# Forms of w_up's result split into high and low parts where they are made, and loaded back as both parts into the tiles that w_down's matmuls read

## What is computed

```python
h2 = rmsnorm(x, norm_mlp_g)
f = relu(einsum('btd,df->btf', h2, w_up))          # 2048 -> 8192
x = x + einsum('btf,fd->btd', f * f, w_down)       # 8192 -> 2048
y = rmsnorm(x, norm_final_g)
```

## Time and profile before

| | before |
|---|---|
| median of three runs | 1854.97 us |
| profiled execution, its own time | 1855.15 us |
| its span | 1853.1 us |
| TensorE busy | 1814.2 us (98%) |
| VectorE busy | 1477.5 us (80%) |
| ScalarE busy | 923.8 us (50%) |
| q1 (weights) | 186.86 MB, 32.6% of 16 engines |
| q0 (POOL's) | 99.18 MB, 18.7% of 16 engines |

### The profile page before, as it was taken

How to read it: one execution, slowest core, us unless ns; L and a number is a source line. 1 busy time by engine, 2 the same in 40 slices (tenths; PEclk the granted TensorE clock), 3 DMA queues, 4 the chain that set the end, 5 groups by cost and what they waited for, 6 DMA issues and landing times. The chain is left out here.

```text
span 1853.1 us, 38289 instructions
## 1 busy us (share of the span) xinstructions
PE 1814.2 (98%) x15016; PEld 1805.6 (97%) x15016; DVE 1477.5 (80%) x2028; ACT 923.8 (50%) x1316; POOL 131.8 (7%) x222
## 2 busy tenths in 40 slices
PE   7999999999999999999999999999999999999997
PEld 6999999999999999999999999899999999999997
DVE  7777785445488888888888888888888888889886
ACT  6545533333344544454454455555555555555554
POOL 2000000200000001000000000110000000000100
PEclk9999999999999999999999999999999999999999
DMA  8333233444345345444444542887666766767632
GB/s 278 97 96 92 91 97 92 127 142 139 113 149 174 133 154 177 151 155 141 166 142 145 174 133 90 246 241 203 182 185 186 199 179 182 198 161 208 206 103 93
DMA packets 209420, 288.21 MB, mean 156 GB/s; under 512 B 9389, under 2 KB 185017, under 8 KB 209248
## 3 DMA queue, kind: packets, MB, share of 16 engines
q1 hardware_dynamic: 185344, 186.86, 32.6%
q0 software_dynamic: 23920, 99.18, 18.7%
HBM read 222.00 MB, written 64.53 MB: 155 GB/s over the span
## 5 line engine op out<-in xcount | busy, mean ns | idle before, releaser
L863 PE MATMUL ps<-forms,u_high 128*128 128x260 f32 x1344 | 379.9, 283 | 2.2 <-ACT u_high L1128 1.2
L865 PE MATMUL ps<-forms,u_low 128*128 128x260 f32 x1344 | 379.5, 282 | 0.0
L864 PE MATMUL ps<-forms,u_high 128*128 128x260 f32 x1344 | 379.2, 282 | 0.0
L863 PE MATMUL ps<-forms,d_high 128*128 128x260 f32 x1120 | 317.1, 283 | 3.1 <-DVE d_low L1737 1.4
L865 PE MATMUL ps<-forms,d_low 128*128 128x260 f32 x1120 | 316.1, 282 | 0.0
L864 PE MATMUL ps<-forms,d_high 128*128 128x260 f32 x1120 | 316.1, 282 | 0.0
L863 PEld LDWEIGHTS ps<-forms,u_high 128*128 128x128 f32 x1344 | 253.0, 188 | 2.5 <-ACT u_high L1128 1.4
L864 PEld LDWEIGHTS ps<-forms,u_high 128*128 128x128 f32 x1344 | 253.4, 189 | 0.0
L865 PEld LDWEIGHTS ps<-forms,u_low 128*128 128x128 f32 x1344 | 252.8, 188 | 0.0
L1277 DVE TENSOR_TENSOR w_low<-raw,w_high 128x512 fp32r<-128x512 f32 x160 | 109.0, 689 | 136.9 <-ACT w_high L941 135.7
L863 PEld LDWEIGHTS ps<-forms,d_high 128*128 128x128 f32 x1120 | 210.7, 188 | 5.1 <-issue 4.3
(11 more groups left out here) (305 smaller groups left out, 4380.3 us busy)
## 6 DMA issues: line engine op xcount, KB each, us to landing
even_rows<-in_w_up_dram SPq DMA_DIRECT2D x32, 1024.0 KB, 5.4
odd_rows<-in_w_up_dram SPq DMA_DIRECT2D x32, 1024.0 KB, 5.7
d_even<-in_w_down_dram SPq DMA_DIRECT2D x33, 768.0 KB, 6.7
d_odd<-in_w_down_dram SPq DMA_DIRECT2D x33, 768.0 KB, 5.2
raw<-in_w_in_dram SPq DMA_DIRECT2D x96, 256.0 KB, 2.7
sums_spill<-part_out POOLq DMA_DIRECT2D x40, 520.0 KB, 5.4
scratch<-f_spill POOLq DMA_DIRECT2D x20, 910.0 KB, 7.1
f_spill<-f_out POOLq DMA_DIRECT2D x32, 520.0 KB, 4.6
```

The lines of the kernel that those rows point to most:

```text
L863: pe.matmul(out, wh[:, k, :], xh, start=(PRODUCT_OPENS[r] and k == 0), stop=False, skip_group_check=True)
L864: pe.matmul(out, wh[:, k, :], xl, start=False, stop=False, skip_group_check=True)
L865: mm = pe.matmul(out, wl[:, k, :], xh, start=False, stop=last, skip_group_check=True)
```

## The change

The forms of a pair are split as soon as they are made. In w_up, split_high (ScalarE, at r = 6) writes the high parts of all seven forms into f_high, a view of scratch; split_low (VectorE, at r = 0 two pairs on) subtracts them in place, so that f_out and the sums tiles hold the low parts. For that f_scale and f_sums stand one turn earlier (r = 4 and 5). POOL stores both parts in f_parts_spill, and loads both straight into f_forms[kp % 8], in two pieces (three and four forms). window_high, window_low, their landing tiles and the lists BUILD and FORMS_AT go. The last pair's forms are made in segments 1 to 3 in place of 3 to 6 (SUMS_SEG = 3). What ScalarE's window_high waited for, POOL's load_forms waits for now. Loads of tiles 0 and 1 stand ahead of send_f(30), those of tiles 2 to 7 directly behind it and ahead of the first send_sums, later ones ahead of the sums of the segment that frees their set.

```diff
+PIECES = ((0, 3), (3, FORMS))
...
-SQUARES_AT, SCALE_AT, SUMS_SEG = first_q(3) + 3, first_q(3) + 6, 6
+SQUARES_AT, SCALE_AT, SUMS_SEG = first_q(1) + 3, first_q(1) + 6, 3
...
-        f_dram = nc.dram_tensor("f_spill", (DOWN_KP, P, FORMS, HALF), F32).ap()
+        parts_dram = nc.dram_tensor("f_parts_spill", (DOWN_KP, P, 2, FORMS, HALF), F32).ap()
+        f_high = scratch[:].rearrange("p k (a t) -> p (k a) t", a=2)[:, 0:FORMS, :]
...
+            def load_forms(kp):
                 if kp == 0:
+                    pool.wait_ge(u_lo, UP_Q - PRODUCTS)
+                elif kp == 1:
+                    pool.wait_ge(u_lo, UP_Q)
+                elif kp < D_SETS:
+                    pool.wait_ge(u_used, UP_Q)
                 else:
+                    pool.wait_ge(u_used, first_q(LAST_USE[kp - D_SETS] + 1))
+                pool.wait_ge(split_sent, 16 * (kp + 1))
                 pool.wait_ge(f_out_sent[kp % 2], SENT[kp])
+                for piece, (first, end) in enumerate(PIECES):
+                    pool.dma_start(f_forms[kp % D_SETS][:, :, first:end, :].bitcast(F32),
+                                   parts_dram[kp, :, :, first:end, :]).then_inc(forms_in[kp % D_SETS][piece], 16)
...
             def send_f(m):
                 pool.wait_ge(f_ready, m + 1)
+                to = parts_dram[m, :, 1]
+                pool.dma_start(parts_dram[m, :, 0], f_high).then_inc(split_sent, 16)
+                pool.dma_start(to[:, 0:4, :], f_out[m % 2][:]).then_inc(f_out_sent[m % 2], 16)
...
             for m in range(UP_PAIRS - 1):
                 if m == UP_PAIRS - 2:
-                    load_f(1)
+                    load_forms(0)
+                    load_forms(1)
                 send_f(m)
-                if m == 8:
-                    load_f(0)
+            for kp in range(2, D_SETS):
+                load_forms(kp)
...
+            for seg in range(FIRST_FINAL):
                 if seg == SUMS_SEG:
                     send_f(UP_PAIRS - 1)
+                for kp in range(D_SETS, DOWN_KP):
+                    if LAST_USE[kp - D_SETS] == seg:
+                        load_forms(kp)
+                send_sums(seg)
...
+                        if FIRST_USE[kp] == m - UP_PAIRS and r < 2:
+                            pe.wait_ge(forms_in[kp % D_SETS][r], 16 * (kp // D_SETS + 1))
...
+            def split_high(m):
+
+                act.wait_ge(f_summed, m + 1)
+                act.wait_ge(split_sent, 16 * m)
+                for part, first, end in split_parts(m):
+                    act.activation(f_high[:, first:end, :].bitcast(F32R), part, ACT.Copy).then_inc(split_hi, 1)
...
+                if r == 6 and 1 <= m < UP_PAIRS:
+                    split_high(m - 1)
+                if turn == first_q(SUMS_SEG) + 1:
+                    split_high(UP_PAIRS - 1)
...
+                if r == 0 and 2 <= m <= UP_PAIRS:
+                    split_low(m - 2)
+                if turn == first_q(SUMS_SEG) + 2:
+                    split_low(UP_PAIRS - 1)
...
+                if 1 <= m < UP_PAIRS and r == 4:
+                    f_scale(m - 1)
                 if 1 <= m < UP_PAIRS and r == 5:
-                    f_scale(m - 1)
-                if 1 <= m < UP_PAIRS and r == 6:
                     f_sums(m - 1)
```

More of the change, by code:

```diff
@@ L96, in first_q @@
     return UP_Q + PRODUCTS * seg
[L100 to L116, removed]
-SQUARES_AT, SCALE_AT, SUMS_SEG = first_q(3) + 3, first_q(3) + 6, 6
+for _kp in range(D_SETS, DOWN_KP):
+    assert LAST_USE[_kp - D_SETS] + 1 < FIRST_USE[_kp]
+SQUARES_AT, SCALE_AT, SUMS_SEG = first_q(1) + 3, first_q(1) + 6, 3
 SENT = {}
@@ L361, in build @@
         d_rows_in = [[sem(f"d_{which}_in{b}") for b in range(4)] for which in ("even", "odd")]
-        f_landed = [sem(f"f_landed{b}") for b in range(2)]
-        f_hi, f_lo = sem("f_hi"), sem("f_lo")
+        f_summed, split_hi, split_sent = sem("f_summed"), sem("split_hi"), sem("split_sent")
+        forms_in = [[sem(f"forms_in{kp}_{piece}") for piece in range(len(PIECES))] for kp in range(D_SETS)]
         sums_sent = [sem(f"sums_sent{b}") for b in range(2)]
@@ L386, in form_rows, with split_parts, split_count @@
             return odd_sums[:, 0, :], odd_sums[:, 1, :], odd_sum[:]
+        def split_parts(m):
+            if m == UP_PAIRS - 1:
+                return (f_out[1][:], 0, 4), (end_sums[:], 4, 7)
+            if m % 2 == 0:
+                return (f_out[0][:], 0, 4), (even_sums[:], 4, 7)
+            return (f_out[1][:], 0, 4), (odd_sums[:], 4, 6), (odd_sum[:].unsqueeze(1), 6, 7)
+        def split_count(m):
+            return 2 * m + m // 2
         def blocks_at(q):
@@ L635, in send_sums @@
                                accum_op=ALU.add).then_inc(sums_sent[seg % 2], 16)
-            loaded = 2
-            for seg in range(-1, FIRST_FINAL):
+            for seg in range(FIRST_FINAL):
                 if seg == SUMS_SEG:
                     send_f(UP_PAIRS - 1)
[L641 to L646, removed]
+                for kp in range(D_SETS, DOWN_KP):
+                    if LAST_USE[kp - D_SETS] == seg:
+                        load_forms(kp)
+                send_sums(seg)
             for i, n in enumerate(FINALS):
@@ L654, in _ @@
                 else:
-                    pool.wait_ge(f_hi, 2 * DOWN_KP)
-                    pool.wait_ge(f_lo, 2 * DOWN_KP)
+                    pool.wait_ge(f_out_sent[0], SENT[UP_PAIRS - 2])
+                    pool.wait_ge(f_out_sent[1], SENT[UP_PAIRS - 1])
                 pool.dma_start(x3[n][:].rearrange("p k (a t) -> p (k a) t", a=2), sums_dram[n]).then_inc(x3_in[i], 16)
@@ L1185, in _ @@
             x2_squares(OUT_PAIRS - 1)
[L1186 to L1199, removed]
             def final_steps(i):
@@ L1817, in f_sums, with split_low @@
                 settle()
[L1818 to L1826, removed]
+                dve.tensor_tensor(s4, a12, s2, ALU.subtract).then_inc(f_summed, 1)
+            def split_low(m):
+                dve.wait_ge(f_summed, m + 1)
+                for n, (part, first, end) in enumerate(split_parts(m)):
+                    dve.wait_ge(split_hi, split_count(m) + n + 1)
+                    if end == FORMS:
+                        settle()
+                    ins = dve.tensor_tensor(part.bitcast(F32R), part, f_high[:, first:end, :], ALU.subtract)
+                    if end < FORMS:
+                        step(ins)
+                ins.then_inc(f_ready, 1)
             def pair_final(i):
@@ L1872, in _ @@
                     f_sums(UP_PAIRS - 1)
-                for part in range(2):
-                    if turn - 2 - part in FORMS_AT:
-                        window_low(FORMS_AT[turn - 2 - part], part)
                 if seg > FIRST_FINAL and r == 3:
```

33 lines of the change are left out of this document (4 added, 29 removed).

## The result

| | before | after |
|---|---|---|
| median of four runs each | 1855.41 us | 1872.44 us |
| lowest to highest | 1853.54 to 1857.82 | 1871.62 to 1873.49 |
| profiled execution (span) | 1855.15 (1853.1) | 1872.58 (1870.8) |

The change makes the kernel slower: ratio 1.0094 (95% interval 1.0081 to 1.0107), some 17 us. The forecast was 1876 in 1863 to 1890.

What follows compares the result with a forecast made beforehand. The prediction took TensorE, busy 1814.2 of 1853.1 us, as the bound, with VectorE limiting for a while early in w_down. Its terms: 1855.15 + 25 - 4 + 0 = 1876 us, range 1863 to 1890.

Steps and rivals of the forecast that it cites:

- w_up: 0: In w_up, the added splits fit VectorE's free 2.8 us a pair, 2.2 wanted, so TensorE loses 0 us.
- The queue: +25: At the seam, 14.9 MB in POOL's queue ahead of segment 0's sums delay the copy waiting for them: +25 us.
- the copy that was named: ScalarE's copy of C11 at r = 5 of segment 2, forecast at 1211.5 against 1186.35 before.
- Given back: -4: Between segments 2 and 7, TensorE catches up 6.2 us less a 2 us stall in segment 3: 4 us returned.
- The stop in segment 3: In w_down, pair 31's f_sums and split now stand in segment 3 on VectorE: 2 us of stall.
- Near the end: 0: Near the end of w_down, 3.6 us of idle may shrink by 1, collisions may take 1: 0.
- possible collisions of double loads: In w_down, two tiles free at once put 3.7 MB in q0; collisions may take 1 us in the forecast.
- rival 1: Later collisions after segments 7, 15, 23 and 31, 3 to 4 us each: 1890 us; chance 0.12.
- Rival 2: At the seam, the sums overtake the loads in q0, and segment 3 waits for rows: 1863 us; chance 0.08.
- rival 3: w_up doesn't hold the splits; 0.5 us a pair lost, 16 us on top: 1891 us; chance 0.06.
- rival 4: Segment 0's sums land before 1186.35 and only VectorE's relief is left, faster: 1849 us; chance 0.04.
- a fifth of the rate: In w_down, q1 with its 1 KB packets gets a fifth beside q0, 85 GB/s, of 399 GB/s together.

Runs made afterwards that it cites:

- e10: e8 with the loads of tiles 2 to 7 together at the end of w_up, the same bytes: 1870.14 us, 1.0084 to the kernel before.
- e1: The changed kernel with only the high parts of tiles 2 to 7 loaded, 5.6 MB less in POOL's queue: 1861.96 us.
- e2: The changed kernel with loads of tiles 2 to 7 issued in pairs between the sums of segments, the same bytes: 1869.72 us.
- e8: The changed kernel with tiles 1 and 30 by the old way, tiles 4 to 7 loaded one a segment, pair 31 in segments 3 to 6: 1846.70 us.
- e6: The changed kernel with tiles 1, 4 to 7, 30 and 31 by the old way, pair 31 in segments 3 to 6: 1859.03 us.
- e3: The kernel before plus six unread stores of a form set, 11.2 MB, in POOL's queue at the end of w_up: 1875.30 us.

## Why the prediction was right, step by step

**w_up: 0.** This was right. TensorE is busy 646.47 us against 646.67, and VectorE 19.14 us in a pair of 20.14 where 19.4 was foreseen. The free 2.8 us were really there, in VectorE's waits, and the two helpers moved a turn earlier fill them.

**The queue: +25.** Measured were 24.6, at the copy that was named: 1210.94 for 1211.5. The last load landed at 1208, the sums behind it at 1210.9. 14.9 MB in order at 397 GB/s with the rows beside them is what the queues show, and the row share was 72 GB/s where 85 had been taken. One link of the chain was wrong. The sums of segment 0 were to be issued before 1180 and left at 1189.21, because segment 1's rows were asked for at 1174.4 and took 8.0 and 11.6 us, and VectorE could not finish the turn before. The landing was not moved by it, since the queue was still ahead of them; the e10 run, where they left at 1178.69, has its copy at 1208.35. But the wait of TensorE came in pieces. Only 8.0 of the 24.6 us are ScalarE's wait for the sums; when it came to the copy it was already 16.6 us behind. The number held because the sums landed last. TensorE was idle for 22.7 us between 1165 and 1215, where some 30 were to be short; the rest of the shortfall is slow matmuls (granted clock 0.70 in this stretch). And e1 and e2 show the second door: take the sums out of the wait and the rows hold TensorE up instead. The forecast had said that the term is hardly touched by how the queues share; it had not said that it is also hardly touched by which of the two is waited for.

**Given back: -4.** Measured 4.8 (24.6 at segment 2, 19.8 at segment 7). The stop in segment 3 is there, 1.45 and 0.52 us at 1219.95 and 1222.14, the 2 us foreseen. That the term came out so near is partly luck, as two things which I did not have nearly cancel. The copy is a poorer mark than I took it for: TensorE stood further ahead of it than in the kernel before. From 1212.82 to segment 7's copy it was busy 58.34 us; less the 1.5 us of slow matmuls below that is 56.8, some 474 matmuls at 0.120 us where 507 had been counted (the traces have 470 here, and 502 between the two copies of before). The 33 fewer save 4 us; against them stand 1.9 us of waiting from the copy to 1212.82 and the 1.5 us of slow matmuls.

**Near the end: 0.** Mis-sized by 1.8: idle time went from 3.6 to 1.3 us in the last 180, and the lag of the copies from 19.8 to 18.0. I had let possible collisions of double loads eat the relief. There are none. This is also the answer to rival 1: from 1250 to 1650 TensorE has no idle time at all, although two tiles are loaded together after segments 7, 15, 23 and 31.

Together: 24.6 - 4.8 - 1.8 = 18.0, less 0.3 in the closing part, is the 17.7 us between the two spans, for the 21 that I had put down. Rival 1 leaned on the earlier trace rows, where q1 "stood still" beside q0: the rows had been asked for only at 1179.16, so that window shows how late they started, not how they fare later. Rival 2 (sums overtaking) has the earlier trace rows and now the 21.7 us against it, and 29.6 in e10; rival 3 (w_up) and rival 4 (faster) are excluded by the windows. Rival 4 asked for a faster q0; what made a kernel faster (e8) was fewer bytes in it at that moment.

## What to carry to other kernels

- Work moved off a busy engine here became bytes in a queue. Before making such a change, list what stands behind those bytes in the same queue, and who waits for it: 14.9 MB at 397 GB/s are 37.5 us in which a 0.5 MB store behind them can't land.
- A prefetch is to be issued when it is needed less its own time, not as soon as its buffer is free. The same bytes one a segment gave 1846.70 us, together 1870.14, and the former kept the DMA engines busier.
- Where two queues share the engines, look at both ends of the share: curing one wait (the sums, e2) gave the other (the rows) nearly the whole of it. In the same way two delays at one place can hide each other: mending tile 1 and pair 30 alone brought some 2 us, with the loads spread as well some 26.

## What the runs showed that was not expected

**The clock falls after a stop, and the price is on the path.** Windows of the kernel after, columns as above (the eighth number is the granted clock):

```profile
1187.50:1192.00 4.50, 4.50 (x21) 4.50 (x22) 3.25 (x9) 3.66 (x8) 0.90 (x1) 0.50 1.04 400
...
1213.00:1216.00 3.00, 3.00 (x15) 3.00 (x16) 2.93 (x8) 1.12 (x2) 0.00 (x0) 0.50 0.72 222
1223.00:1233.00 10.00, 10.00 (x85) 10.00 (x85) 8.71 (x16) 4.86 (x9) 1.43 (x3) 1.00 0.99 320
```

A granted clock of 0.50 is the lower level, 1.2 GHz, and 1.00 is 2.4 GHz. TensorE had stood still for 7.08 us before 1212.82 and then ran at the lower level until 1216.2: 3.00 us for 15 matmuls, 0.20 each, where the last window has 10 us for 85, 0.12 each. From 1212.82 to 1216.20 it is 3.38 us for 16 matmuls, which at 0.12 would be 1.9: the 1.5 us used above. There were three more such stretches between 1168 and 1203, but by the order of the waits they lay among waits that would have lasted anyway (this was not tried by itself). The kernel before has one, at 1177.7 to 1181.1, behind the stops of 0.83 and 1.58 us of the earlier trace rows; e8 has none, though it stopped for 1.22 and 1.34 us (clock 1.00 in its window, 0.98 in that of before).

**Packets one for one.** Where both queues move data their counts are the same within 1.5% (1464 to 1460, 620 to 621, 836 to 848 in the earlier trace rows). So the hardware queue got 72 GB/s beside packets of 4.4 KB and 30 GB/s beside 12.8 KB. (The larger ones are stores, the others mostly loads; the size alone was not varied.) The prediction had taken a fifth of the rate from the earlier trace rows, a share for one pair of packet sizes. And rows start late beside a full q0: those asked for at 1174.44 had moved 5 packets by 1178, those of the earlier trace rows, asked for at 1179.16, 8 by 1183.5. Why is open.

**What stays open.** Why the rows of segment 3 are late in e6 (tile 4's load is beside them, but was not moved alone), and which of the two waits, sums or rows, sets e3's time: the copy's wait of 0.16 us says the rows, on one profile. What tile 1 and pair 30 cost each was not tried apart.
